# A causal convolution's taps: part of one of TensorE's channel tiles moved to ScalarE and GpSimd, begun earlier

## What is computed

```python
def _conformer_conv(h, w_in, b_in, dw, dw_b, ln_g, ln_b, w_out, b_out):
    ab = h @ w_in + b_in
    a, b = jnp.split(ab, 2, axis=-1)
    u = a * jax.nn.sigmoid(b)
    u = lax.conv_general_dilated(u, dw[:, None, :], (1,), padding=[(CONV_WIDTH - 1, 0)],
        dimension_numbers=("NWC", "WIO", "NWC"), feature_group_count=D_MODEL) + dw_b
    u = jax.nn.silu(_layernorm(u, ln_g, ln_b))
    return u @ w_out + b_out
```

## Time and profile before

| what | us |
|---|---|
| median of 3 runs (961.45 to 963.29) | 962.78 |
| the profiled execution: its own time | 963.62 |
| its span, first to last instruction | 961.8 |
| TensorE busy in the span | 954.0 |
| VectorE busy | 767.9 |
| ScalarE busy | 492.2 |
| GpSimd busy | 68.8 |

### The profile page before, as it was taken

One profiled execution on the slowest core, in us unless ns is written; L12 is line 12 of the kernel. 1 busy time (PEld: TensorE's weight loads), 2 busy tenths in 40 slices (PEclk: granted clock), 3 DMA queues, 4 the chain that ended last, 5 costly groups with the idle time before them and its releaser, 6 DMA issues.

```text
span 961.8 us, 12442 instructions
## 1 busy us (share of the span) xinstructions
PE 954.0 (99%) x4475; PEld 788.9 (82%) x4475; DVE 767.9 (80%) x1445; ACT 492.2 (51%) x777; POOL 68.8 (7%) x75
## 2 busy tenths in 40 slices
PE   8999999999999999999999999999999999999998
PEld 6888888888988888888888888888778888888887
DVE  6758787879969978787888878786877888878882
ACT  6635344465765535344453535354778854444441
POOL 0200000000621000000000000000433100000000
PEclk9999999999999999999999999999999999999999
DMA  8974636452835664636445554544524545464521
GB/s 287 351 316 148 245 136 251 178 214 95 286 131 192 210 239 145 248 136 248 182 155 219 192 202 175 217 159 191 175 89 147 191 182 201 155 229 164 210 96 44
DMA packets 29085, 183.53 MB, mean 191 GB/s; under 512 B 3440, under 2 KB 3568, under 8 KB 8816
## 3 DMA queue, kind: packets, MB, share of 16 engines
q1 hardware_dynamic: 26784, 176.17, 48.7%
q0 software_dynamic: 2112, 6.70, 2.1%
q10 hardware_dynamic: 144, 0.07, 0.1%
HBM read 181.88 MB, written 1.05 MB: 190 GB/s over the span
## 4 chain that ended last, share of the span: by engine, by line
PE 96%; DVE 1%; ACT 1%; DMA 1%; issue 0%; POOL 0%; ACTq 0%
PE pg L505 17%; PE pg L509 17%; PE pg L511 17%; PE acc L505 13%; PE acc L509 13%; PE acc L511 13%; PE acc L699 3%; PE pt L594 1%; DVE w_lo L1322 1%; PE acc L809 1%; DMA raw<-in_units 1%; PE pt L828 1%; DMA first<-in_first 0%; ACT w_hi L904 0%; PE pt L790 0%; PE pt L623 0%
## 5 line engine op out<-in xcount | busy, mean ns | idle before, releaser
L1322 DVE TENSOR_TENSOR w_lo<-raw,w_hi 128x1024 fp32r<-128x1024 f32 x316 | 371.6, 1224 | 16.7 <-ACT w_hi L904 15.3
L904 ACT CAST w_hi<-raw 128x1024 fp32r<-128x1024 f32 x316 | 313.1, 1046 | 14.8 <-DMA raw<-in_units 14.8
L505 PE MATMUL pg<-w_hi,a_hi 128*128 128x512 f32 x720 | 282.6, 392 | 0.0
L511 PE MATMUL pg<-w_hi,a_lo 128*128 128x512 f32 x720 | 280.3, 389 | 0.0
L509 PE MATMUL pg<-w_lo,a_hi 128*128 128x512 f32 x720 | 280.2, 389 | 0.0
L1444 DVE STREAM_TRANSPOSE mix<-hs 32x128 f32<-32x128 f32 x592 | 179.2, 303 | 8.9
L505 PEld LDWEIGHTS pg<-w_hi,a_hi 128*128 128x128 f32 x720 | 135.2, 188 | 29.0 <-issue 1.4
L511 PEld LDWEIGHTS pg<-w_hi,a_lo 128*128 128x128 f32 x720 | 135.1, 188 | 28.1
L509 PEld LDWEIGHTS pg<-w_lo,a_hi 128*128 128x128 f32 x720 | 135.2, 188 | 27.1
L1436 DVE SCALAR_TENSOR_TENSOR hs<-pg,rstd,hs 128x256 f32<-128x256 f32 x80 | 38.4, 484 | 105.3 <-ACT hs L949 105.3
L949 ACT ACTIVATE hs<-pg,rstd 128x256 f32<-128x256 f32 x80 | 37.9, 475 | 164.5 <-PE pg L511 164.5
(11 more groups left out here) (153 smaller groups left out, 666.6 us busy)
## 6 DMA issues: line engine op xcount, KB each, us to landing
raw<-in_units SPq DMA_DIRECT2D x158, 1024.0 KB, 5.2
diags<-in_conv_diags SPq DMA_DIRECT2D x12, 512.0 KB, 4.4
raw<-in_units SPq DMA_DIRECT2D x8, 256.0 KB, 6.1
diags<-in_conv_diags POOLq DMA_DIRECT2D x4, 512.0 KB, 20.4
gain<-in_ffn_norm POOLq DMA_DIRECT2D x3, 512.0 KB, 4.4
xs<-in_x SPq DMA_DIRECT2D x4, 256.0 KB, 5.8
gain<-in_mix_norm POOLq DMA_DIRECT2D x2, 512.0 KB, 7.0
xg<-in_conv_b_in POOLq DMA_DIRECT2D x2, 512.0 KB, 4.2
```

What stands on the lines that cost most here:

```text
L505: mm = pe.matmul(dst[j], stat_hi, m_hi, start=first, stop=False)
L511: mm = pe.matmul(dst[j], stat_lo, m_hi, start=False, stop=last)
L904: nc.scalar.copy(w_hi[n % RING][:, cols], raw[n % RAW][:, cols]).then_inc(hi_done, 1)
L1322: nc.vector.tensor_tensor(w_lo[n % RING][:, cols], raw[n % RAW][:, cols], w_hi[n % RING][:, cols].bitcast(F32), ALU.subtract).then_inc(lo_ ...
```

## The change

The first of TensorE's tiles, tile 4 (groups 0 and 1), is split by the rows of the filter. TensorE keeps one half of the diagonals for each of the two groups (rows 16 to 30 of `conv_dw`, 8 matmuls in place of 16), and ScalarE and GpSimd compute rows 0 to 15 and the bias of that tile from a second copy of its signal (`more_up`), in a second running pair (`more_sum`): eight more pairs of products, seven sums and a fold. The result is added in PSUM: TensorE multiplies it with the identity into the place where the groups' turned sums already lie (`add_more`).

ScalarE's products of tile 3 begin after `place(1)`, not after chunk 3, and its whole order from chunk 1 on is written out anew: roundings of u+8 to u+11 come between the products, and u+12 is rounded after the layer norm. VectorE's running sums go to PSUM from delay 9 on. Its two rests of u+10 leave the end of the taps for the place after the layer norm where the rests of u+11 were, and those follow them. The statistics of tiles 4 and 5 are taken last. One of the four gain loads moves behind GpSimd's sums.

```diff
@@ -76,7 +76,15 @@
 LAG = SHIFTS - 1
-HALVES = 2 * GROUPS
+SPLIT = SHIFTS - 1
+MORE_PAIRS = (W - SPLIT) // 2
+PRODUCTS_AT = [13, 15, 18, 20, 23, 24, 24]
+HALF0 = [0, 1] + [2 * g - 2 for g in range(2, GROUPS + 1)]
+HALVES = HALF0[GROUPS]
@@ -350,11 +358,23 @@
             return (pg, pt)[j // 2][:, j % 2, :].rearrange("p (i n) -> p i n", i=2)
-        pair_sum = sil.rearrange("p t n -> p (t n)")
+        pair_sum = gain[:, 0, 2 * T:4 * T]
+        more_sum = sil.rearrange("p t n -> p (t n)")
+        more_up = gain[:, 0, 0:PAD + T]
+        more = hid[:, 0, :]
         def pair_at(p):
-            return gain[:, 1, p % 2 * 2 * T:(p % 2 + 1) * 2 * T] if p else pair_sum
+            if p == 0:
+                return pair_sum
+            return gain[:, 1, p % 2 * 2 * T:(p % 2 + 1) * 2 * T] if p != PAIRS else more_sum
+        def products_of(p):
+            if p < PAIRS:
+                return range(2 * p, min(2 * p + 2, W)), min(2 * p + 2, W)
+            return range(2 * (p - PAIRS), 2 * (p - PAIRS) + 2), W + 2 * (p - PAIRS + 1)
@@ -417,12 +437,18 @@
             def sum_pair(p):
-                n = min(2, W - 2 * p) * T
-                pool.wait_ge(product_done, min(2 * p + 2, W))
+                to = pair_sum if p < PAIRS else more_sum
+                delays, products = products_of(p)
+                n = len(delays) * T
+                pool.wait_ge(product_done, products)
...
                     pool.wait_ge(pair_summed, p - 1)
-                nc.gpsimd.tensor_tensor(pair_sum[:, 0:n], pair_sum[:, 0:n], pair_at(p)[:, 0:n], ALU.add).then_inc(pair_summed, 1)
+                nc.gpsimd.tensor_tensor(to[:, 0:n], to[:, 0:n], pair_at(p)[:, 0:n], ALU.add).then_inc(pair_summed, 1)
+            def fold(to, of, summed):
+                pool.wait_ge(pair_summed, summed)
+                nc.gpsimd.tensor_tensor(to, of[:, 0:T], of[:, T:2 * T], ALU.add).then_inc(pair_summed, 1)
@@ -432,6 +458,7 @@
             nc.gpsimd.memset(up2[:, :, 0:LAG], 0.0).then_inc(pad_zero, 1)
+            nc.gpsimd.memset(more_up[:, 0:PAD], 0.0).then_inc(pad_zero, 1)
@@ -463,10 +490,9 @@
                     pool.dma_start(b_out, conv_b_out[0].partition_broadcast(P)).then_inc(b_out_loaded, 16)
-                if kind == "turn" and a < 4 and a != CONV:
-                    if a:
-                        pool.wait_ge(xg_ready, 4 * a)
+                if kind == "turn" and CONV < a < 4:
+                    pool.wait_ge(xg_ready, 4 * a)
@@ -474,10 +500,14 @@
                         sum_pair(p)
-                    pool.wait_ge(pair_summed, PAIRS - 1)
-                    nc.gpsimd.tensor_tensor(cv[:, DVE_TILES, :], pair_sum[:, 0:T], pair_sum[:, T:2 * T], ALU.add) \
-                        .then_inc(pair_summed, 1)
-                    pool.wait_ge(pair_summed, PAIRS)
+                    fold(cv[:, DVE_TILES, :], pair_sum, PAIRS - 1)
+                    for p in range(PAIRS + 1, PAIRS + MORE_PAIRS):
+                        sum_pair(p)
+                    pool.wait_ge(u_turned, 4)
+                    fold(more, more_sum, PAIRS + MORE_PAIRS - 1)
+                    pool.wait_ge(pair_summed, PAIRS + MORE_PAIRS)
+                    load_gain(a + 1)
@@ -689,15 +719,15 @@
                         pe.wait_ge(cv_taken, g - 1)
-                    for h in (2 * g, 2 * g + 1):
+                    for h in range(HALF0[g], HALF0[g + 1]):
...
                         for i in range(SHIFTS // 2):
-                            b = h % 2 * (SHIFTS // 2) + i
+                            b = (h - HALF0[g]) * (SHIFTS // 2) + i
                             mm = pe.matmul(sums(g), diags[:, h % DIAG_RING, i * P:(i + 1) * P],
-                                           up2[:, g, LAG - b:LAG - b + P], start=b == 0, stop=b == SHIFTS - 1)
+                                           up2[:, g, LAG - b:LAG - b + P], start=b == 0, stop=b == (HALF0[g + 1] - HALF0[g]) * (SHIFTS // 2) - 1)
@@ -705,7 +735,22 @@
                     at = k % 2 * P + half * PC
-                    return pe.transpose(by_parity(k // 2)[:, :, at:at + PC], cv2[:, g, :], ident)
+                    dst = by_parity(k // 2)[:, :, at:at + PC]
+                    if k == VK + 1:
+                        return pe.matmul(dst, cv2[:, g, :], ident, start=False, stop=False, is_transpose=True)
+                    if k == VK:
+                        return pe.matmul(dst, cv2[:, g, :], ident, start=g == 0, stop=False, is_transpose=True)
+                    return pe.transpose(dst, cv2[:, g, :], ident)
+                def add_more():
+                    pe.wait_ge(pair_summed, PAIRS + MORE_PAIRS)
+                    for i in range(2):
+                        mm = pe.matmul(by_parity(VK // 2)[:, i, 0:P], more.rearrange("p (m i) -> p i m", i=2)[:, i, :], ident,
+                                       start=False, stop=i == 1)
+                    return mm
@@ -728,9 +773,8 @@
                 taps(5)
-                for g in range(3):
+                for g in range(4):
                     turn_group(g)
-                turn_group(3).then_inc(c_turned, 1)
@@ -740,6 +784,7 @@
                 turn_group(7).then_inc(c_turned, 1)
+                add_more().then_inc(c_turned, 1)
@@ -1036,6 +1081,8 @@
                         else:
+                            if k == VK:
+                                nc.scalar.copy(more_up[:, PAD:PAD + T], src)
@@ -1049,47 +1096,71 @@
                 def take(g):
-                    act.wait_ge(diag_used, 2 * (g + 1))
-                    nc.scalar.activation(cv2[:, g, :], sums(g), ACT.Identity, bias=group_b[:, g:g + 1]).then_inc(cv_taken, 1)
+                    act.wait_ge(diag_used, HALF0[g + 1])
+                    if g < 2:
+                        nc.scalar.copy(cv2[:, g, :], sums(g)).then_inc(cv_taken, 1)
+                    else:
+                        nc.scalar.activation(cv2[:, g, :], sums(g), ACT.Identity, bias=group_b[:, g:g + 1]).then_inc(cv_taken, 1)
                 def products(p0, p1):
-                    if p0 == 0:
-                        act.wait_ge(chunk_out, 2 * (c0 + chunks))
                     for p in range(p0, p1):
-                        if p >= 3:
+                        k = DVE_TILES if p < PAIRS else VK
+                        if p == 0:
+                            act.wait_ge(u_placed, DVE_TILES + 1)
+                        if p == PAIRS:
+                            act.wait_ge(chunk_out, 2 * (c0 + chunks))
+                        elif p >= 3:
                             act.wait_ge(pair_summed, p - 2)
-                        for j in range(2 * p, min(2 * p + 2, W)):
-                            dst, src = pair_at(p)[:, j % 2 * T:(j % 2 + 1) * T], up[:, DVE_TILES, j:j + T]
-                            weight = chan[:, DVE_TILES, j:j + 1]
+                        for j in products_of(p)[0]:
+                            dst = pair_at(p)[:, j % 2 * T:(j % 2 + 1) * T]
+                            src = (up[:, k, :] if k < VK else more_up)[:, j:j + T]
+                            weight = chan[:, k, j:j + 1]
                             if j == 0:
-                                mm = nc.scalar.activation(dst, src, ACT.Identity, bias=chan[:, DVE_TILES, W:W + 1], scale=weight)
+                                mm = nc.scalar.activation(dst, src, ACT.Identity, bias=chan[:, k, W:W + 1], scale=weight)
...
                 enter(s)
-                for c in range(chunks):
-                    if c:
-                        tick(u + 2 * c, 0, lambda: place(c - 1))
-                    tick(u + 2 * c + 1)
-                    if c < chunks - 1:
-                        sigmoids(c)
-                sigmoids(chunks - 1)
-                products(0, 3)
+                act.wait_ge(pad_zero, 3)
+                tick(u + 1)
+                sigmoids(0)
+                tick(u + 2, 0, lambda: place(0))
+                tick(u + 3)
+                sigmoids(1)
+                round_half(u + 8, 0)
+                place(1)
+                products(0, 2)
+                round_half(u + 8, 1)
+                products(2, 4)
+                sigmoids(2)
+                products(4, 5)
+                round_half(u + 9, 0)
+                place(2)
+                products(5, 7)
+                round_half(u + 9, 1)
+                products(7, 9)
+                sigmoids(3)
+                products(9, 10)
                 take(0)
-                products(3, 4)
+                products(10, 11)
                 take(1)
-                place(chunks - 1)
-                products(4, 6)
+                round_half(u + 10, 0)
+                products(11, 12)
+                place(3)
+                products(12, 13)
...
                     take(g)
-                    products(min(3 * g, PAIRS), min(3 * g + 3, PAIRS))
+                    products(PRODUCTS_AT[g - 2], PRODUCTS_AT[g - 1])
+                    if g == 2:
+                        round_half(u + 10, 1)
                     if g in (5, 6):
```

(22 more changed lines are left out.)

## The result

| | before | after |
|---|---|---|
| median of 22 runs each | 962.25 (961.06 to 963.81) | 964.69 (961.66 to 966.49) |
| profiled execution | 963.62, span 961.8 | 964.79, span 963.0 |

The ratio is 1.0022, with a 95% interval of 1.0016 to 1.0029: the kernel after is **slower by 2.1 us** on the ratio (2.4 between the medians), at the edge of the 0.2% that the prediction called no change.

What follows compares the result with a forecast made beforehand. TensorE, 96% of the chain, was taken to bound the kernel. -3.57 + 0.7 + 1.0 + 2.2 + 0.35 = +0.7 us, taken as +0.6 on the median 962.78: 963.4, own range 962.5 to 965, with rivals 960.0 to 965.2.

Steps and rivals of the forecast that it cites:

- the upper end of the bounds: VectorE's taps with both inputs in SBUF: each GpSimd sum holds one tap for its whole 1.27 us.
- 16 taps off: TensorE's list in the convolution: 16 matmuls fewer at 0.2234 us each, 3.57 us off.
- wait at `turn_u(2)`: TensorE waits 1.0 us there, since held VectorE instructions end `glu(2)` 1.8 late, less the slack of 0.8.
- wait at `turn_u(3)`: TensorE, there at 245.2, waits 2.2 us for VectorE, which reaches `glu(3)` at 245.0 and ends it at 247.3.
- statistics: Ahead of the layer norm: three pairs instead of two are left when the last turns come, +0.7 us.
- small waits: Group 2 starts 0.2 us late behind products; the turn of tiles 0 and 1 waits 0.15 for VectorE.
- Rival A: Convolution: SBUF taps pass beside GpSimd's sums, so VectorE is hardly late; about -2.3 us, 960.4, faster; chance 0.25.
- rival B: TensorE's clock falls after the wait at `turn_u(3)`: 2.0 us more, 965.5, slower; chance 0.10.
- the case with a chance of 0.12: Whole kernel slower than before by over 0.2%, above 964.7 us.
- that with 0.63: Whole kernel within 0.2% of before, between 960.85 and 964.7 us.
- Rival C: Diagonals for group 3's taps land late behind the load of u+12: +0.9 us on the forecast, 964.3; chance 0.08.
- After the layer norm ... all at nothing: Behind the norm, VectorE's two more rests, ScalarE's later rounding of u+12 and the moved gain load cost nothing.

Runs made afterwards that it cites:

- after_again: The kernel after, unchanged, measured again under another name: 964.59 us, ratio 1.0016 to before.
- fill: The kernel after with eight unused 512-column matmuls on TensorE ahead of `turn_u(3)`, where it had waited: 964.32 us, ratio 1.0016 to before.
- early_only: The kernel after without the split of tile 4 (TensorE keeps all its taps), early products and roundings kept: 970.98 us, ratio 1.0084 to before.
- early_gains_late: The kernel after without tile 4's split, diagonals ahead of u+12's load, u+9's rests behind the norm, two gain loads held until the last diagonals are used: 965.86 us.
- rest9_late: The kernel after with VectorE's two rests of u+9 put behind the layer norm and the diagonals ahead of u+12's load: 962.71 us, ratio 1.0002 to before.

## Why the prediction came out as it did

**What held.** Taps in SBUF exclude GpSimd's sums, as the upper end of the bounds had it, and VectorE is late at both turns. Shifted to the first turn of before (+0.79), `glu(2)` starts at 230.5 (forecast 230.6), the taps' records at 241.5 (241.6), VectorE's last tap at 269.1 (269.2). Term by term, in us:

| term | forecast | measured |
|---|---|---|
| 16 taps off | -3.57 | -3.57 |
| wait at `turn_u(2)` | +1.0 | +0.9 (0.72 idle; the turn 23.60 behind the first, 22.72 before) |
| wait at `turn_u(3)` | +2.2 | +2.0 (the turn comes 5.62 after the taps, 7.15 before, and 3.57 less to do) |
| statistics | +0.7 | +0.66 |
| small waits | +0.35 | +0.3 |
| sum | +0.7 | +0.37 |
| TensorE's clock | not in the forecast | +1.64, in part of the executions |

The measured column is that of after_again; the terms add to 0.3, beside the 0.37 of the whole stretch. Part of the closeness is luck: two steps of the forecast stand lower than their own terms. The holds of 1.3, 1.2 and 1.25 less 1.63 of idleness are 2.1 and not the 1.8 with which it goes on at `glu(2)`; it was 1.65 (229.67 + 0.79 against 228.81), since the two held taps took 2.07 more and not 2.45. And from 232.9, with 7.2, 1.1, 2.35, 0.6 and 1.2, VectorE would reach `glu(3)` at 245.3 and not at 245.0; it was 244.8. Rival A, taps that pass beside sums, is excluded by 2.94 us against 0.87 for the same two taps.

**What failed** is one step, at the fourth turn: "it waits 2.2" was the end of the account in the forecast, with the clock at full behind it, and the fall of the clock was rival B with a chance of 0.10. The wait is as forecast, 1.9, and the clock falls behind it in some 9 to 21 of 33 executions; the size, 2 us, was near the 1.64. The argument against B, that no slice of the clock row shows a mark of the idle times that there are, was weak three times. None of those idle times was longer than 0.62 in the stage. A slice of 24 us at 0.93 still prints as a 9. And the row had missed a slow stretch before: in the profile of before the matmuls of the earlier trace rows, which B's own price was taken from, start 0.43 us apart (8.28 and 8.71), while the granted clock reads 1.00 from 8 to 12; in after the same 0.43 (9.53 and 9.96) stands with 0.50. An event that depends on chance within one kernel belongs in the forecast with its share: 0.7 and half of 1.6 are 1.5, and so about 964.3. The median of 964.69 is inside the range, near its upper end and 1.3 above the forecast, and without a fall after's executions have 963.1; the ratio of 1.0022 falls in the case with a chance of 0.12 rather than in that with 0.63. That fill's time shows none of what its clock keeps leaves open how much of the 2.1 us is the fall's.

The Trainium skill (TensorE: Matmul & The Clock Gate, Part 1, "The HAM clock gate") says that the gate watches in windows that run freely and aren't reset when a kernel starts, so that the same kernel can show different counts of slow matmuls. The two profiles of after are in line with that and don't show it: with a wait of 1.91 the clock fell, with one of 1.88 it did not.

**Rival C** has no place in after: no bracket before its taps names a DMA. early_only shows the mechanism at its full size. Two things differ in after: it has two of sixteen halves of diagonals less to bring, and GpSimd's further sums keep the gains back. early_gains_late shows the second to be worth the last two waits; what the first is worth by itself is not shown.

**"After the layer norm ... all at nothing"** held for after (B 686.55), and rest9_late shows how near it was: with two half rests more, VectorE is 1.06 late at 299 us.

## What to carry to other kernels

Work taken off TensorE is a gain only where the operand behind it is ready sooner too: here 3.57 us of taps turned into 2.9 us of waits for VectorE, since GpSimd's sums, begun earlier to make room for a part of them, shut out VectorE's instructions with two SBUF inputs. Where a forecast ends in a new wait of TensorE of one or two microseconds, price the clock behind it as a part of the sum, and take a second profile before believing that it falls or that it doesn't. The gain came back by moving VectorE's free work (the rests) into its own idle times, and each such move has to be followed to the next stage's entry.
